# Dilated attention: silu of the gate from a tanh on ScalarE and one two-step VectorE operation, in place of an exponential, an addition, a reciprocal and a product

## What is computed

```python
def mixer_dilated(u, w_in, w_out, rel_bias):
    q, k, v, gate = jnp.split(u @ w_in, 4, axis=-1)       # each 18 heads x 64 = 1152 wide
    ...
    for g, (window, dil) in enumerate(DIL_GROUPS):        # (128,1) (512,4) (2048,16), 6 heads each
        hs = slice(g * HEADS_PER_GROUP_A, (g + 1) * HEADS_PER_GROUP_A)
        o, l = dilated_window_attention(q[:, :, hs], k[:, :, hs], v[:, :, hs], rel_bias[:, hs], window, dil)
        ...
    wts = jax.nn.softmax(jnp.stack(lses, axis=0), axis=0)  # over the three groups
    o = jnp.concatenate([outs[g] * wts[g][..., None] for g in range(len(DIL_GROUPS))], axis=2)
    y = o.reshape(B, S, WIDTH_A) * jax.nn.silu(gate)
    return y @ w_out
```

## Time and profile before

| | us |
|---|---|
| three runs | 3977.55, 3975.87, 3971.01 |
| their median | 3975.87 |
| the profiled execution, its own time | 3970.35 |
| its span, first to last instruction | 3968.2 |
| TensorE busy in the span | 3758.5 |
| VectorE busy in the span | 2294.6 |
| ScalarE busy in the span | 1453.7 |
| GpSimd busy in the span | 1916.7 |

### The profile page before, as it was taken

The page is one execution under the profiler, slowest core; times in us unless marked ns, Lnnn a source line. Parts: engine busy times, 40 slices in busy tenths (PEclk is TensorE's granted clock), DMA queues, the critical chain, the costliest instruction groups (busy, mean ns, idle before and its releaser), DMA issues.

```text
span 3968.2 us, 49652 instructions
## 1 busy us (share of the span) xinstructions
PE 3758.5 (95%) x19015; PEld 3105.0 (78%) x19015; DVE 2294.6 (58%) x3586; ACT 1453.7 (37%) x2930; POOL 1916.7 (48%) x1675
## 2 busy tenths in 40 slices
PE   5899998999999999999898999999999898999998
PEld 4778787787888877787577888888877576888887
DVE  5453536564777765534638777634544638777533
ACT  1123223134666662225534333212225534333211
POOL 1414131562333324422525788986322526788975
PEclk8999998999999999999999999999999999999999
DMA  5322222322000003110132222543110132222543
GB/s 178 113 69 77 72 59 70 107 74 47 10 6 9 9 6 117 58 32 22 32 102 88 80 80 83 185 146 133 65 40 20 32 105 85 80 83 83 184 159 124
DMA packets 245062, 309.84 MB, mean 78 GB/s; under 512 B 38533, under 2 KB 156693, under 8 KB 244826
## 3 DMA queue, kind: packets, MB, share of 16 engines
q1 hardware_dynamic: 212152, 231.87, 18.9%
q10 hardware_dynamic: 32674, 74.80, 5.5%
HBM read 252.96 MB, written 51.53 MB: 77 GB/s over the span
## 4 chain that ended last, share of the span: by engine, by line
PE 74%; DVE 15%; ACT 4%; issue 3%; POOL 2%; DMA 1%; ACTq 0%; DVEq 0%; SPq 0%; POOLq 0%
PE ps L130 70%; PE ps L133 4%; DVE ml_p L142 3%; DVE cst_sm L153 3%; ACT thi L136 2%; DVE da_sg L159 1%; DVE tlo L142 1%; DVE f_ta L150 1%; ACT ml_o L136 1%; DVE f_tb L150 1%; POOL mix_z L142 1%; ACT tfi L136 0%; POOL wlo L142 0%; DVE da_am L150 0%; POOL mlo_z L142 0%
## 5 line engine op out<-in xcount | busy, mean ns | idle before, releaser
L139 POOL CAST whi<-wst 128x512 fp32r<-128x512 f32 (+2 forms) x508 | 421.5, 830 | 1288.0 <-DMA wst<-in_a_w_in 400.9
L142 POOL TENSOR_TENSOR wlo<-wst,whi 128x512 fp32r<-128x512 f32 (+2 forms) x634 | 936.4, 1484 | 40.8
L130 PE MATMUL ps<-whi,thi 128*128 128x512 f32 (+3 forms) x1816 | 711.5, 392 | 20.1 <-POOL wlo L142 8.0
L130 PE MATMUL ps<-whi,tlo 128*128 128x512 f32 (+3 forms) x1816 | 686.6, 378 | 0.0
L130 PE MATMUL ps<-wlo,thi 128*128 128x512 f32 (+3 forms) x1816 | 685.9, 378 | 0.0
L130 PEld LDWEIGHTS ps<-whi,thi 128*128 128x128 f32 x1816 | 345.7, 190 | 83.0 <-POOL wlo L142 9.7
L130 PEld LDWEIGHTS ps<-wlo,thi 128*128 128x128 f32 x1816 | 345.6, 190 | 58.1 <-issue 4.1
L130 PEld LDWEIGHTS ps<-whi,tlo 128*128 128x128 f32 x1816 | 344.5, 190 | 58.2
L130 PE MATMUL ps<-thi,whi 128*128 128x512 f32 x856 | 343.7, 402 | 34.0 <-POOL wlo L142 24.2
L130 PE MATMUL ps<-tlo,whi 128*128 128x512 f32 x856 | 340.2, 397 | 0.0
L130 PE MATMUL ps<-thi,wlo 128*128 128x512 f32 x856 | 340.1, 397 | 0.0
(11 more groups left out here) (393 smaller groups left out, 8181.0 us busy)
## 6 DMA issues: line engine op xcount, KB each, us to landing
wst<-in_w_down SPq DMA_DIRECT2D x140, 256.0 KB, 3.3
wst<-in_w_up SPq DMA_DIRECT2D x126, 256.0 KB, 2.9
scr_h<-f_tb SPq DMA_DIRECT2D x44, 512.0 KB, 3.9
wst<-in_w_in SPq DMA_DIRECT2D x80, 256.0 KB, 2.7
wst<-in_a_w_in SPq DMA_DIRECT2D x72, 192.0 KB, 2.4
wst<-in_ada_w SPq DMA_DIRECT2D x48, 256.0 KB, 4.8
da_am<-in_ada_w SPq DMA_DIRECT2D x48, 256.0 KB, 2.7
f_T2lw<-scr_h SPq DMA_DIRECT2D x48, 256.0 KB, 3.8
```

What stands on the lines that cost most here:

```text
L130: return self.none if self.e is None else self.e.matmul(*a, **k)
L139: return self.none if self.e is None else self.e.tensor_copy(*a)
L142: return self.none if self.e is None else self.e.tensor_tensor(*a)
```

## The change

The gate's function on ScalarE becomes tanh of half the gate, and VectorE's three operations on `asg` become one of two steps, (`asg` + 1) times the gate from PSUM. The missing factor one half goes into the output of the block, which becomes an operation of two steps as well: attention output times 0.5 times `asg`. Nothing else is edited.

```diff
-                q.activation(self.asg[:, j % 2, :], ps[:, B.of(key), 0:384], ACT.Exp, scale=-1.0).then_inc(*S.up("gexp", (g, j)))
+                q.activation(self.asg[:, j % 2, :], ps[:, B.of(key), 0:384], ACT.Tanh, scale=0.5).then_inc(*S.up("gexp", (g, j)))
...
                 q.wait_ge(*S.at("gexp", (g, j)))
-                q.tensor_scalar(a, a, 1.0, None, ALU.add).then_inc(*S.up("v_seq"))
-                q.wait_ge(*S.last("v_seq"))
-                q.reciprocal(a, a).then_inc(*S.up("v_seq"))
-                q.wait_ge(*S.last("v_seq"))
-                q.tensor_tensor(a, ps[:, B.of(key), 0:384], a, ALU.mult).then_inc(*B.free(key, "evac_v"))
+                q.stt(a, a, 1.0, ps[:, B.of(key), 0:384], ALU.add, ALU.mult).then_inc(*B.free(key, "evac_v"))
...
-                q.tensor_tensor(y[:, 0:384], ps[:, B.of(key), 0:384], self.asg[:, j % 2, :], ALU.mult).then_inc(
+                q.stt(y[:, 0:384], ps[:, B.of(key), 0:384], 0.5, self.asg[:, j % 2, :], ALU.mult, ALU.mult).then_inc(
                     *B.free(key, "evac_v"))
```

## The result

| | before | after |
|---|---|---|
| median, us | 3976.71 (4 runs, 3971.01 to 3986.97) | 3938.94 (4 runs, 3934.95 to 3940.71) |
| the profiled execution, us | 3970.35 | 3940.71 |
| its span, us | 3968.2 | 3938.9 |
| TensorE busy, us | 3758.5 | 3742.0 |
| VectorE busy, us | 2294.6 | 2230.0 |

The changed kernel takes 0.9908 of the time of before, with a 95% interval of 0.9893 to 0.9922, so it is faster by 0.8 to 1.1%. A second set of runs of the same kernel (the first experiment) gave 3942.44. The two spans differ by 29.3 us, and it is this difference that the traces can explain.

What follows compares the result with a forecast made beforehand. TensorE's own chain bounds the kernel (busy 3758.5 of 3968.2 us), with waits for VectorE at group ends in the mixer. Stalls 16.9 plus clock 9.8 give 26.7 us: 3975.87 to 3949.2 us, range 3940 to 3963.

Steps and rivals of the forecast that it cites:

- The operations: VectorE's gate in the mixer: new operation 557 ns, successors start 2.99 us earlier; block output and tanh taken at no cost.
- The stalls: TensorE's waits for VectorE in the mixer, mostly at group ends: 16.9 of 23.2 us would go.
- The one to be kept: The wait at 642.02 us, where VectorE's list runs beside GpSimd's weight splitting: 2.5 us of it would remain.
- The clock: Behind stalls at the group ends the granted clock would stay at the upper level, returning 9.8 us.
- The rival by which it stays low: From 650 us small products could keep the clock low, so only stalls count: 3959.0 us; chance 0.20.
- The step that failed: 157 to 265 us, blocks with full filler: TensorE busy for all 108.00 us, so six gates there were priced at nothing.
- the 13 reciprocals on the chain: Gate reciprocals of 2.55 us on the mixer's chain, 100 to 720 us: 33 us, 5.4%, 13 of 24 gates.
- the sum: Total gain forecast in the mixer: 16.9 us of stalls and 9.8 us of clock, 26.7 us.
- The forecast for the profiled execution itself: The whole kernel's profiled execution, 3970.35 us before, would take 3943.6 us.
- all stalls close: Rival: every mixer stall closes, the one at 642.02 too, and the whole clock returns: 31.6 us, 3944.3; chance 0.12.
- another wait takes over: Rival: at group ends ScalarE's exponential or the transfer into `da_yr` is late instead; unchanged at 3975.87 us; chance 0.10.
- The table loads: Rival: tanh brings two loads of 1283 ns per gate on ScalarE, 61.6 us; 4010.8 us fully on path; chance 0.03.

Runs made afterwards that it cites:

- the first experiment: The changed kernel timed again without any edit, in more rounds: 3942.44 us, ratio 0.9914 to the kernel before.
- the last run: Changed kernel with GpSimd's splits of output projection weights in three parts: four behind block 4, three behind 5, four behind 6; 3937.74 us, ratio 0.9905.
- the filler alone: Kernel before, with twelve unread matmuls ahead of the last product with the values in groups 0 and 1; one run, 3979.38 us.

## Why the prediction was right, and where its size was off

*The operations.* Priced at 557 ns, the new one takes 551; its hold on its successor is 0.47 us as put (627.51 to 627.98). The block's output and the tanh cost nothing. All of it as worked out.

*The stalls.* 16.9 us were to go and 16.2 went, by the sum of all rows. The prediction's "14 in number" left out the row of eleven waits that name the gate's product, shown above. The one to be kept was put at 2.5 us and is 2.83, and the list behind it at 6.46 us and is 6.18. Its cause was argued then and is shown now: the wait followed GpSimd's splits from block 4 to 5 to 6 as these were moved, at 2.83, 5.19 and 4.77 us, and fell to 1.04 and 1.06 us when the splits stood between the lists. The rule of "SBUF — State Buffer" (Who interferes with whom) in the Trainium skill, which the prediction leaned on, agrees with the direction: the product of small SBUF tiles takes 0.57 us for three alone and 1.21 to 1.87 beside a split, while the new gate operation with its operand in PSUM stays within 548 to 554 ns in all places. The scaling of `da_yr` took 2.50 us beside the splits in the changed kernel and 1.02 at 649.24 in the last run, when the last split had ended.

*The clock.* 9.8 us were to come back and 9.3 did, by the same stretches. The rival by which it stays low is refuted by the windows behind all three group ends. Its argument that the stalls from 650 to 685 us are short was a misreading: waits of 1.95, 1.57 and 3.30 us stand there. For groups 0 and 1 the traces of the other runs bear the link out. The three kernels with the old hold at these ends (before, the new gate only in the full blocks, the reciprocal put back) have waits of 2.39 to 3.11 us for the copy there, and the clock over the 5 us behind is 0.50 to 0.66 at all six places; the eight with the new gate there have no such wait, and their clock is 1.00 from 260 to 300 and from 450 to 500 us. That it is the idle time, and not something else of the old gate, the filler alone argues, in one run at the end of group 1. At the end of group 2 the wait of 2.91 us in the run with the reciprocal left the clock up, so there the link is not shown.

*The step that failed* is the one by which a block with all its filler gains nothing: TensorE was "busy for all of 108.00 us", and the six gates in that stretch were priced at no cost. These blocks gained 4.3 us by their own starts; with the new gate in them alone it was 4.0 by the starts and 3.5 by the medians. The windows and the sum of waits count a row of four loads as one piece of work, and waits of some 0.1 to 0.3 us inside it are invisible there. Two signs were in views that the prediction draws on: the eleven waits for the gate's product all stand in these blocks, and of the 13 reciprocals on the chain four, at 574.84, 588.39, 602.33 and 616.27 us, are theirs. With them the sum would have been 26.7 + 4.3 = 31.0 us, against 30.4 measured in the mixer. Outside the full blocks the mixer gained 26.1 us, where the sum had 26.7. The mechanism was right and a term of the sum, put at zero, was too small.

*The median.* The kernel before ran 3969.86 to 3989.31 us in the 20 runs of the second set, and the changed one 3939.36 to 3947.24. The start of the mixer alone lies between 170.2 and 173.3 us in the traces here, with nothing changed ahead of it. The profiled run of before lay 6.4 us below the median of its first set's four runs and the profiled run of after 1.8 above its own, which is why the medians differ by 37.8 and the spans by 29.3. The forecast for the profiled execution itself, 3943.6, lies 2.9 us above its 3940.71.

*The rivals.* That all stalls close fell with the 2.83 us. That another wait takes over fell too: behind the copy and the reductions no wait above 1.2 us came up in the changed kernel but the one named. The table loads do not occur, and where they were forced they cost an eighth (mixer) to a fifth (span) of the 61.6 us and not all of it.

## What to carry to other kernels

An operation of VectorE that is off TensorE's path nearly everywhere can still be worth its place where filler runs out: nine of 24 gates gave 30 of 33 us here, and each microsecond of stall brought somewhat more than half of another in clock (16.2 and 9.3), on average and not behind every wait. A stretch in which TensorE counts as busy without a gap is no proof that nothing is late in it; compare the distance of the same event from block to block, and look at the rows of several loads that have become longer. A row of waits that names the very operation to be changed is worth a look even where it is small. When a wait is left, find which other engine works beside the list that is late before moving anything, and count all that this engine does until it stops: moving part of it only moves the wait.

## What the runs showed of the hardware that was not expected

The clock does not answer to the length of a wait alone. Before, a wait of 2.13 us at 269.70 left it at 1.00 for the next 10 us:

```profile
269.70 0.29 PEld L130 LDWEIGHTS ps<-da_k,da_q 64*128 64x128 f32 x2 [2.13 <-DVE da_y L156]
...
270.00:275.00 5.00, 5.00 (x33) 3.78 (x31) 2.26 (x11) 2.03 (x10) 0.00 (x0) 1.00 0.11 41
```

In the run with filler, one of 2.19 us at the same place of the program was followed by 0.71 and then 0.50 until 290 us, and that block took 19.98 us in place of 13.60. Later in these two runs a wait of 1.42 us at one place (460.65 and 469.04) was followed by 1.00 before and by 0.66 over 470 to 475 us with filler. What decides stayed open. In the three-part run two waits of 1.04 and 1.06 us left the clock at 1.00, and so did the one of 2.91 us with the reciprocal put back.

Loads of function tables between operations that TensorE seldom waits for cost far less here than their time: 1.28 us each on ScalarE, 0.16 us each at the end of the mixer and 0.25 at that of the kernel.
